# Two moves beside the latent projections: a weight panel's high part from ScalarE to GpSimd, and the decay's running sums to an earlier place on VectorE

## The reference, cut to what matters

```python
proj = h @ w_in
u, v_m, o_pre, i_pre, f_pre, c_q, c_kv, k_r = jnp.split(proj, idx, axis=-1)
...
ig = (i_pre + b_igate).transpose(0, 2, 1)
fg = (f_pre + b_fgate).transpose(0, 2, 1)
hm = mlstm_chunkwise(q_m, k_m, v_h, ig, fg)      # logf = log_sigmoid(fg); b = cumsum(logf); running maxima of i - b
y_m = jax.nn.sigmoid(o_pre) * rmsnorm_2(hm, m_out_g)
...
q_a = (rmsnorm_2(c_q, cq_norm_g) @ w_uq)          # 4 heads of 192
kv = (rmsnorm_2(c_kv, ckv_norm_g) @ w_ukv)        # 4 heads of 128 + 128
q_nope = rmsnorm_2(q_a[..., :NOPE_DIM], ...); k_nope = rmsnorm_2(k_nope, ...)
o_a = causal_block_attention(q_full, k_full, v_a)
return jnp.concatenate([y_m, y_a], axis=-1) @ w_out
```

## Time and profile before

| | |
|---|---|
| three runs, us | 1870.56, 1871.62 (median), 1872.0 |
| profiled execution, us | 1872.21 |
| its span, first to last instruction, us | 1870.1 |
| mean granted TensorE clock | 0.999 |
| TensorE busy, us | 1835.2 |
| GpSimd busy, us | 1369.4 |
| VectorE busy, us | 922.2 |
| ScalarE busy, us | 756.7 |

### The profile page before, as it was taken

One profiled execution on the slowest core, in us unless ns is written; L12 is line 12 of the kernel. 1 busy time (PEld: TensorE's weight loads), 2 busy tenths in 40 slices (PEclk: granted clock), 3 DMA queues, 4 the chain that ended last, 5 costly groups with the idle time before them and its releaser, 6 DMA issues.

```text
span 1870.1 us, 26050 instructions
## 1 busy us (share of the span) xinstructions
PE 1835.2 (98%) x9519; PEld 1549.3 (83%) x9519; DVE 922.2 (49%) x1806; ACT 756.7 (40%) x1459; POOL 1369.4 (73%) x1211
## 2 busy tenths in 40 slices
PE   7999999999999999999999999999999999999999
PEld 6888888888878888878888888887678988888887
DVE  6677777772117875355403411827663465203410
ACT  4577777764027773242102110567644532001200
POOL 8766666698854559989888988753434689888885
PEclk9999999999999999999999999999999999999999
DMA  7322222223343232423332333222023223332342
GB/s 222 113 68 68 68 69 68 69 68 91 90 116 87 52 87 89 159 68 90 92 110 90 90 101 101 69 63 68 24 68 113 91 68 90 106 96 90 92 111 68
DMA packets 213612, 165.69 MB, mean 89 GB/s; under 512 B 14478, under 2 KB 209873, under 8 KB 213122
## 3 DMA queue, kind: packets, MB, share of 16 engines
q1 hardware_dynamic: 208134, 149.32, 27.4%
q10 hardware_dynamic: 5372, 14.98, 2.4%
HBM read 161.11 MB, written 7.37 MB: 90 GB/s over the span
## 4 chain that ended last, share of the span: by engine, by line
PE 56%; POOL 4%; DVE 2%; issue 2%; ACT 2%; POOLq 0%; DVEq 0%; ACTq 0%
PE bank L410 43%; PE bank L486 4%; POOL w_lo L3264 2%; PE bank L1599 1%; PE bank L436 1%; POOL w_hi L3256 1%; PE bank L1623 1%; POOL x_features L761 1%; PE bank L3014 1%; PE bank L1821 1%; PE bank L1800 1%; PE bank L1810 0%; PE bank L2663 0%; PE bank L1609 0%; DVE arena L639 0%
## 5 line engine op out<-in xcount | busy, mean ns | idle before, releaser
L3264 POOL TENSOR_TENSOR w_lo<-w_raw,w_hi 128x512 fp32r<-128x512 f32 (+1 forms) x572 | 721.9, 1294 | 201.0 <-ACT w_hi L1446 191.5
L3256 POOL TENSOR_TENSOR w_hi<-w_raw,one 128x512 fp32r<-128x512 f32 (+1 forms) x428 | 441.6, 1063 | 212.5 <-PE bank L410 193.5
L410 PE MATMUL bank<-h_hi,w_hi 128*128 128x512 f32 x952 | 376.9, 396 | 0.8 <-POOL w_lo L3264 0.6
L410 PE MATMUL bank<-h_hi,w_lo 128*128 128x512 f32 x952 | 371.8, 391 | 0.0
L410 PE MATMUL bank<-h_lo,w_hi 128*128 128x512 f32 x952 | 371.1, 390 | 0.0
L410 PE MATMUL bank<-a_hi,w_hi 128*128 128x512 f32 x832 | 325.8, 392 | 0.4 <-DVE a_lo L553 0.3
L410 PE MATMUL bank<-a_hi,w_lo 128*128 128x512 f32 x832 | 324.0, 389 | 0.0
L410 PE MATMUL bank<-a_lo,w_hi 128*128 128x512 f32 x832 | 323.7, 389 | 0.0
L410 PEld LDWEIGHTS bank<-h_hi,w_lo 128*128 128x128 f32 x952 | 178.7, 188 | 38.9
L410 PEld LDWEIGHTS bank<-h_hi,w_hi 128*128 128x128 f32 x952 | 178.9, 188 | 35.3 <-issue 1.4
L410 PEld LDWEIGHTS bank<-h_lo,w_hi 128*128 128x128 f32 x952 | 179.0, 188 | 33.6
(11 more groups left out here) (506 smaller groups left out, 3009.2 us busy)
## 6 DMA issues: line engine op xcount, KB each, us to landing
w_raw<-in_w_ff SPq DMA_DIRECT2D x32, 1024.0 KB, 5.6
w_raw<-in_w_in SPq DMA_DIRECT2D x31, 1024.0 KB, 5.4
w_raw<-in_w_mlp_in SPq DMA_DIRECT2D x16, 1024.0 KB, 5.4
w_raw<-in_w_mlp_out SPq DMA_DIRECT2D x16, 1024.0 KB, 5.8
w_raw<-in_w_in SPq DMA_DIRECT2D x26, 512.0 KB, 4.5
w_raw<-in_w_ssd_out SPq DMA_DIRECT2D x8, 1024.0 KB, 5.7
bias_rows<-bias_row ACTq DMA_DIRECT2D x1, 4096.0 KB, 15.8
w_raw<-in_w_attn_out SPq DMA_DIRECT2D x4, 1024.0 KB, 5.2
```

The lines of the kernel that those rows point to most:

```text
L410: mm = pe.matmul(bank[:, 0:ntok], a, b[:, koff + k, 0:ntok], start=(k == 0 and n == 0), stop=(k == L.kb - 1 and n == 2))
L3256: pool.tensor_tensor(w_hi[:, slot, part], raw[:, slot, part], one[:].broadcast_to([P, n]), ALU.mult).then_inc(split_hi, 1)
L3264: ins = pool.tensor_tensor(w_lo[:, slot, part], raw[:, slot, part], w_hi[:, slot, part].bitcast(F32), ALU.subtract)
```

## The change

`L_gate_m[1]` leaves the list `HIGH_BY_ACT`, so GpSimd makes its high pieces too, and ScalarE's `split_high_act(act, L_gate_m[1])` goes. The first three instructions of `gate_rows_dve` (L2394, L2397, L2398) become `gate_sums_dve`, which VectorE issues ahead of the key sums; the other three stay where they were.

```diff
-        HIGH_BY_ACT = list(range(L_ssd[1][0].p0, L_gate_ssd.p0)) + ... + [L.p0 for L in (L_va, L_low, L_vb, *L_gate_m)] + ...
+        HIGH_BY_ACT = list(range(L_ssd[1][0].p0, L_gate_ssd.p0)) + ... + [L.p0 for L in (L_va, L_low, L_vb, L_gate_m[0])] + ...
...
-        def gate_rows_dve(dve):
+        def gate_sums_dve(dve):
             r2, r3, r4, r5 = ROW
             dve_link(dve.memset(DECAY_ROWS, 0.0))
             dve.wait_ge(ml["rows_in"], 1)
             zero = cmask[0:4, 0:1].broadcast_to([4, S])
             dve_link(dve.tensor_tensor_scan(r4, r5, zero, 0.0, ALU.add, ALU.add))
             dve_link(dve.tensor_tensor(r2, r2, r4, ALU.subtract))
+
+        def gate_rows_dve(dve):
+            r2, r3, r4, r5 = ROW
             dve_link(dve.tensor_tensor_scan(r3, r2, r2, 0.0, ALU.max, ALU.max))
             dve_link(dve.tensor_tensor(r5, r4, r3, ALU.add))
             dve_link(dve.tensor_scalar(r3, r3, -1.0, None, ALU.mult))
...
             tokens_act(act, L_gate_m[0], 0, lambda t: OM[:, t, 0:256], ACT.Sigmoid)
-            split_high_act(act, L_gate_m[1])
             for i in range(2 * T):
                 k_block_act(act, i)
...
             q_norm_dve(dve, T - 1)
+            gate_sums_dve(dve)
             for i in range(2 * T):
                 k_sums_dve(dve, i)
             gate_rows_dve(dve)
```

More of the change, by code:

```diff
@@ L1427, in ssd_stage_pe @@
             pe_panel(pe, L_ssd_out, 0, 0, a_x, ks=range(0, 2 * GROUPS - 2))
-        HIGH_BY_ACT = list(range(L_ssd[1][0].p0, L_gate_ssd.p0)) + [L_attn[1][0].p0, L_attn[1][1].p0] + [L_mlp[0][0][0].p0 + 1, L_u.p0 + 1] + [L.p0 for L in (L_va, L_low, L_vb, *L_gate_m)] + [L_out2.p0 + 2, L_out2.p0 + 3] + list(range(L_kx.p0, L_vx.p0 + 2))
+        HIGH_BY_ACT = list(range(L_ssd[1][0].p0, L_gate_ssd.p0)) + [L_attn[1][0].p0, L_attn[1][1].p0] + [L_mlp[0][0][0].p0 + 1, L_u.p0 + 1] + [L.p0 for L in (L_va, L_low, L_vb, L_gate_m[0])] + [L_out2.p0 + 2, L_out2.p0 + 3] + list(range(L_kx.p0, L_vx.p0 + 2))
         high_by_act, low_by_dve = sem("high_by_act"), sem("low_by_dve")
```

## The result

The changed kernel took 1875.41 us, median of 16 runs (1874.22 to 1877.37), against 1871.53 for the kernel before in 16 runs: ratio 1.002, 95% interval 1.0014 to 1.0027, 3.9 us more. The forecast was 1876.5, 4.9 more than the 1871.62 of before. The profiled execution took 1875.13 us with a span of 1873.2 and a mean granted clock of 0.996 (before: 1872.21, 1870.1, 0.999).

What follows compares the result with a forecast made beforehand. TensorE, busy 1835.2 of 1870.1 us, was taken to bound the kernel. L2625 coming 3.2 us later plus 1.7 us of fallen clock made +4.9 us, 1876.5 against the median 1871.62; range 1872.4 to 1878.6.

Steps and rivals of the forecast that it cites:

- The turns: VectorE from 1277.4: each two-input instruction waits for one whole GpSimd piece; last query norm 4.1 us late.
- Rival (b): Half the contention: VectorE's two-input instructions evenly slowed by 2; 1872.6 us, with the clock 1874.3; chance 0.13.
- The buffers: Four key-square buffers: ScalarE's square of block 4 waits for the late first key sum, 1288.18 instead of 1284.08, 4.1 us later.
- The last wait: L2625 follows the gate half without waiting for VectorE, 1298.64 instead of 1295.47; 3.2 us later, through to the end.
- The clock: TensorE's 7.2 us stop ahead of L2545 lets its clock fall to half rate for 3.4 us, costing 1.7 us.
- the other place: TensorE at 1166 to 1172 in the profile before: 3.4 us at 1.2 GHz, taken as the fall's length.
- The sum: Whole kernel: +3.2 for the late L2625 and +1.7 for the clock, +4.9 us; 1876.5 against the median.
- likeliest case: The forecast itself, late L2625 plus clock fall: 1876.5 us, own range 1875.5 to 1878; chance 0.58.
- rival (a): TensorE's clock holds, all else as forecast without the 1.7 us: 1874.8 us, +0.17%; chance 0.13.
- (c): VectorE's sums run at their times alone, L2625 at 1293.0: 2.5 us less, 1869.1 us; chance 0.09.
- (d): L2394 also waits (+1.5 us), or the clock stays down longer in the gate half: 1878.6 and up; chance 0.07.

Runs made afterwards that it cites:

- the kept-busy one: The full change with TensorE repeating turned bank 3's four transposes fifteen times during its stop: 1873.74 us, against 1875.41 for the full change.
- the seventh kernel: Kernel before, plus GpSimd making the high part, eight key-square buffers, masked queries behind the key norms, sums in their old place: 1868.41 us, ratio 0.9986.
- the last two: Kernel before with GpSimd's high part, eight buffers, masked queries behind the key norms: sums in old place 1868.41 us, sums early 1868.71 us.

## Why the prediction was right

**The turns.** This was the step on which everything rested, and it came out nearly to the hundredth. In before's time L2495 ended at 1278.99, L2330 at 1280.04, L2331 at 1281.09, L2332 at 1282.28, L2334 at 1283.71; worked out were 1278.99, 1280.04, 1281.09, 1282.27 and 1283.70. GpSimd had started at 1277.46 (1277.4). L2394 ran beside GpSimd, as I let it. The scan and L2398 ended at 1285.91 and 1287.52 (1285.97, 1287.70). The halved pieces show the cause: the wait goes with the length of the other engine's instruction. Rival (b) is out, and with it the reading of the two engines as sharing evenly. The rule of the Trainium skill that I set beside it (SBUF — State Buffer, Who interferes with whom: the one that starts first keeps the shared ports for its whole instruction) agrees with these rows, 1.40 us against 0.72 with halved pieces. The section says this of VectorE's two-port modes; of an instruction with two inputs it says that it contends with GpSimd for an exclusive lock, and these rows have the whole instruction for that kind too.

**The buffers.** ScalarE went on at 1288.00 in before's time (1288.18 worked out). One reading beside this was wrong: before, the first key sum did not come 1.8 us after its square. It began as the square ended (1281.36, the square from 1280.91 to 1281.33), and the 1.77 in its row is VectorE's wait for the square. It was done at 1281.78, 2.3 us ahead of the square of block 4; the sum in the prediction does not use the 1.8. Eight buffers took the 4 us away with VectorE just as late, so the key-square buffers are the place where it was handed on.

**The last wait.** L2628 had no wait for VectorE, as said; the stop alone put it 3.0 us late (3.2 said). The last decay row ended at 1293.61 in before's time and not at 1296.1, because GpSimd waited for the same bank and was idle beside the decay rows. That these 3.2 us go through to the end held but for the 0.4 us at L1609.

**The clock.** It fell, as said, and cost 1.2 us at the place and 1.7 in the medians (1.7 said for the place). I had let the slow time begin with TensorE's work; in the profiled execution it began near 1287, four microseconds before TensorE went on, so only some 3 us of work ran slowly. The 3.4 us taken over from the other place were not the length of this fall: it lasted 6.8 us (0.75, 0.50, 0.50 and 0.54 over four times 2 us, worked out as in the prediction). That the term came near is luck: a fall twice as long, half of it in the stop, where it cost nothing. The rule of the Trainium skill (TensorE: Matmul & The Clock Gate, Part 1) that activity releases the throttled clock agrees: the clock read 0.50 behind the stop, and with the repeated transposes it reads 1.00.

**The sum.** 3.9 us for 4.9: the terms at L2628 were 2.96 + 1.18 = 4.1 for 3.2 + 1.7, and 3.7 was left at L410 and at the end. The term that was mis-sized most is the clock's, by 0.5 us. The number alone would not have spoken for the forecast: 1875.41 is just below the likeliest case's own range (1875.5 to 1878) and nearer to rival (a), 1874.8, than to 1876.5. It is the rows that do. What remains open is the size of the clock's share in the medians, 1.7 or 2.0 us where the place gains 1.2; the clock also falls elsewhere, and not at the same places in each profiled execution (near 1168 in that of before, near 807 and 1168 in that of the full change, near 84 in the kept-busy one).

**The rivals.** (a), the clock holds: out (0.50 from 1288 to 1292). (c), the gain as drawn: it exists, 2.6 us at L2626 in the seventh kernel, but only with the buffers and GpSimd's later work changed too. (d): L2394 did not wait, and the clock was back after the first six products of the gate half.

## What to carry to other kernels

When work is moved to GpSimd, play through VectorE's two-input instructions beside it, one whole GpSimd instruction each, and ask what is queued behind the last of them; and follow a late small instruction to the buffer it frees, for the number of buffers decides whether another engine stops. Two moves that are each harmless can meet in one such buffer. A stop of TensorE costs more than its length when the clock is still down behind it, 1.2 us here on top of 3.0.

## What the runs showed of the hardware

The clock fell also at short stops: 2.80 us in the kernel with GpSimd's part alone (granted clock 0.85, 0.50, 0.80 from 1286 to 1292), and in the kernel with eight buffers behind a stop of 1.24 us and the thin transposes at L2629. The stops of 1.17 and 1.19 us ahead of bank 4, in the kernel before and in the last two, left it at 1.00. A VectorE tensor_scalar with one input (the last decay row) took 1.15 us beside GpSimd and 0.42 alone, while reductions with one input kept 0.42 in both.
